# One decoder layer on one core: scan chunks in one block, choice, scores and time steps in one block, constants behind the first weights

## The reference

```python
z, xbc, dt_raw, q_raw, k_raw, v_raw, iq_raw, ik, iw_raw, g_a, g_b = split_cols(rms_norm(x, norm1_g) @ w_in)
# (A) state space branch: depthwise causal conv of 4 taps and silu on x/B/C, then
dt = softplus(dt_raw + dt_bias); A = -exp(a_log)
# prompt, in chunks of 128 positions, h carried from chunk to chunk, per group g and head r:
acum = cumsum(dt * A); lmat = exp(where(causal, acum_t - acum_s, -inf)); cb = C @ B.T
y = (cb * lmat * dt) @ x + exp(acum) * (C @ h)
h = h * exp(acum[-1]) + B.T @ (exp(acum[-1] - acum) * dt * x)
# samples: one step, h = h * exp(dt * A) + dt * x * B, y = C . h
y_ssd = group_rms_norm((y + d_skip * x) * silu(z))
# (B) sparse attention: indexer scores pick the keys of each query
score = sum_h iw_h * relu(iq_h . ik) / 8, masked to k_pos <= q_pos
idx = top_k(score, 64 for the prompt, 256 for a sample)
y_att = softmax(q . k[idx] / 8 + rel_bias[bucket(distance)]) @ v[idx]
# merge, then 8 heads x 16 of 16384 single-neuron experts
x = x + (sigmoid(g_a) * (y_ssd @ w_a) + sigmoid(g_b) * (y_att @ w_b)) @ w_out
out = x + peer(rms_norm(x, norm2_g))
```

## Time and profile before

| | |
|---|---|
| median of 3 executions | 1476.19 us (1475.57 to 1476.94) |
| the profiled execution | 1481.15 us, span 1479.5 us |
| busy, share of the span | PE 1257.2 us (85%), DVE 857.2 (58%), ACT 580.8 (39%), POOL 383.9 (26%) |
| moved by DMA | 391.26 MB, mean 264 GB/s |
| mean granted TensorE clock | 0.95 |

### The profile page before, as it was taken

One profiled execution on the slowest core, in us unless ns is written; L12 is line 12 of the kernel. 1 busy time (PEld: TensorE's weight loads), 2 busy tenths in 40 slices (PEclk: granted clock), 3 DMA queues, 4 the chain that ended last, 5 costly groups with the idle time before them and its releaser, 6 DMA issues. The chain is left out here.

```text
span 1479.5 us, 17316 instructions
## 1 busy us (share of the span) xinstructions
PE 1257.2 (85%) x4988; PEld 770.5 (52%) x4988; DVE 857.2 (58%) x2345; ACT 580.8 (39%) x1542; POOL 383.9 (26%) x510
## 2 busy tenths in 40 slices
PE   5997899999677878889989999877778777777776
PEld 4876578777555557758867555322223222222221
DVE  1044369998284334551116867878965667776444
ACT  1153237878383404320004444343343333333343
POOL 1320012222021110010002445443534334333341
PEclk8998999999796889899999999999999999999999
DMA  4563123334289462123337999999999999999995
GB/s 151 172 214 99 58 93 122 111 103 148 100 285 327 149 232 76 29 72 117 112 127 297 420 421 421 421 420 421 421 422 421 421 421 420 421 421 419 421 413 238
DMA packets 80185, 391.26 MB, mean 264 GB/s; under 512 B 13432, under 2 KB 23192, under 8 KB 43744
## 3 DMA queue, kind: packets, MB, share of 16 engines
q0 software_dynamic: 43104, 287.92, 47.5%
q1 hardware_dynamic: 36016, 100.68, 19.9%
q10 hardware_dynamic: 976, 1.61, 0.3%
HBM read 378.43 MB, written 11.60 MB: 264 GB/s over the span
## 5 line engine op out<-in xcount | busy, mean ns | idle before, releaser
L2039 DVE CUSTOM_DVE_ANT_0 pe_uv<-pe_uv,pe_hnat 128x1024 f32<-128x1024 f32 x264 | 322.9, 1223 | 195.4 <-DMA pe_uv<-d_uv,pe_idx 180.5
L1899 POOL DMA_INDIRECT pe_uv<-d_uv,pe_idx x256 | 268.0, 1047 | 398.4 <-PE pe_acc L1776 184.3
L1776 PE MATMUL pe_ph<-pe_uv,pe_dg 128*128 128x512 f32 x512 | 253.0, 618 | 69.8 <-ACT pe_dg L1843 69.8
L1776 PE MATMUL pe_acc<-pe_uv,pe_dg 128*128 128x512 f32 (+1 forms) x544 | 257.8, 610 | 49.3 <-ACT pe_dg L1843 49.3
L181 PE MATMUL pi_ps<-xn,pi_w 128*128 128x264 f32 x944 | 228.3, 399 | 9.5 <-PEq L87 9.5
L1776 PEld LDWEIGHTS pe_ph<-pe_uv,pe_dg 128*128 128x128 f32 x512 | 87.0, 189 | 235.3 <-ACT pe_dg L1843 173.1
L181 PEld LDWEIGHTS pi_ps<-xn,pi_w 128*128 128x128 f32 x944 | 183.5, 198 | 42.8 <-issue 11.3
L1837 ACT ACTIVATE pe_gl<-pe_a 128x1 f32<-128x1 f32 x264 | 53.4, 202 | 379.0 <-DVE pe_a L2039 378.5
L1776 PEld LDWEIGHTS pe_acc<-pe_uv,pe_dg 128*128 128x128 f32 (+1 forms) x544 | 93.7, 184 | 205.0 <-ACT pe_dg L1843 118.2
L1843 ACT ACTIVATE pe_dg<-cst,pe_w 128x128 f32<-128x128 f32 x256 | 102.7, 401 | 8.3
L1840 ACT ACTIVATE pe_w<-pe_gl,pe_gw 128x1 f32<-128x1 f32 x256 | 75.4, 295 | 8.3
(11 more groups left out here) (296 smaller groups left out, 1655.9 us busy)
## 6 DMA issues: line engine op xcount, KB each, us to landing
pi_w<-d_w_in SPq DMA_DIRECT2D x71, 512.0 KB, 3.5
mw_w<-d_w_ab SPq DMA_DIRECT2D x24, 512.0 KB, 3.7
ss_h<-d_state SPq DMA_DIRECT2D x8, 1024.0 KB, 6.9
o_ssm_s<-ss_h SPq DMA_DIRECT2D x8, 1024.0 KB, 7.0
pq_w<-d_wq SPq DMA_DIRECT2D x16, 512.0 KB, 7.7
paged<-d_ck POOLq DMA_DIRECT2D x40, 128.0 KB, 3.3
lg_w<-d_w_in SPq DMA_DIRECT2D x10, 512.0 KB, 6.4
paged<-d_cv POOLq DMA_DIRECT2D x32, 128.0 KB, 4.9
```

What stands on the lines that cost most here:

```text
L1776: mm = pe.matmul(accs[n][0:m, 4 * half:4 * half + 4, :], lhsT, uv[:, r, D_MODEL + half * 512:D_MODEL + (half + 1) * 512], start=False, sto ...
L1899: pool.indirect_dma_start(uv[:, r, :], None, k.d_uv[:], bass.IndirectOffsetOnAxis(ap=src, axis=0)).then_inc(gathered[r], 16)
L2039: dve.tensor_tensor_reduce(uv[:, r, 0:D_MODEL], uv[:, r, 0:D_MODEL], hnat[:, n, :], 1.0, 0.0, ALU.mult, ALU.add, a[:, r:r + 1]).then_inc(d ...
```

## The change

Seven edits, all ahead of the merge:

1. `norm_in` becomes part of `project_attention`. x is loaded in 4 parts with a semaphore each, squared on DVE part by part, summed by PE with a ones tile that DVE fills; ACT loads the root's table with a one-element activation; PE's first tile waits for each normalised chunk, not for all 8. `cst` is loaded behind the first 4 weight tiles, `cx` and the gain from ACT's queue. ACT's six tables and POOL's pages are issued in the same block, so from its start.
2. The z and x/B/C tiles come in a fixed mixed order (7 z, 4 x, 3 z, 28 x, 6 z); the host reorders the weights.
3. `prepare_attention` takes 7 tiles, loads the time steps' three tables, and no longer waits for the stored keys, values and indexer keys; `attend_prompt` does.
4. `choose_prompt`, `score_sample` and `time_steps` become one block, `choose`, with 7 tiles; the widening is one matmul of 256 columns on a table of products that DVE makes. Its scratch and the bias tables of the samples lie in the room of `gate`.
5. `attend_prompt` has 34 tiles, one in each of its 32 steps and two at its tail, and loads the samples' bias tables.
6. `attend_sample`: 16 gate tiles, 4 of them in the key phase at visits 3, 6, 9 and 12, 2 between, 10 over the value visits.
7. `ssd_chunk` twice becomes `scan` once, with 16 groups; chunk 1's transposes and products are made in chunk 0's groups 2 to 7 and in chunk 1's first two, in one PSUM bank, the attention tiles come at every third group.

The core of the diff:

```diff
-N_LAST = 10
+N_LAST, N_KEYS = 16, 4
+COLUMNS = "z" * 7 + "x" * 4 + "z" * 3 + "x" * 28 + "z" * 6
...
 def project_attention(nc, k):
+            for i in range(PARTS):
+                sp.dma_start(k.xT[:, i * WIDE:(i + 1) * WIDE, :], k.d_xT[:, i * WIDE:(i + 1) * WIDE, :]
+                             ).then_inc(x_loaded[i], 16)
+            for n in range(WSLOTS):
+                pj.load(sp, n)
+            sp.dma_start(k.cst[:], k.d_cst[:]).then_inc(c_loaded, 16)
...
+            for c in range(KD):
+                if c % WIDE == 0:
+                    pe.wait_ge(squared, c // WIDE + 1)
+                mm = pe.matmul(sums[:, 0:T], one[:], xsq[:, c, :], start=c == 0, stop=c == KD - 1)
...
-                pj.multiply(pe, n)
+                pj.multiply(pe, n, (lambda c: pe.wait_ge(done, c + 1)) if n == 0 else None)
...
+            act.wait_ge(filled, 2)
+            act.activation(warm[:, 1:2], warm[:, 0:1], ACT.Sqrt).then_inc(warmed, 1)
...
 def prepare_attention(nc, k, tiles):
-            sp.wait_ge(stored, 48)
...
+def choose(nc, k, tiles):
+            k.proj.multiply(pe, tail[0])
+            pe.wait_ge(rectified, len(steps))
...
+            k.proj.multiply(pe, tail[1])
...
+                if b == 1:
+                    pe.wait_ge(diag, TS)
+                if b:
+                    scores(b - 1)
+                if b == 5:
+                    pe.wait_ge(s_weighed, 2)
+                    pe.wait_ge(dA_ready, 1)
+                    pe.matmul(cum[:, 0:NP_], k.tri, k.dA[:, 0:NP_], start=True, stop=True)
...
+            k.proj.multiply(pe, tail[2])
...
+            pe.matmul(px, k.half_of, k.ts["each"][rows, :], start=True, stop=True,
+                      tile_position=(DT_P, 0)).then_inc(widened, 1)
...
+            for step in range(STEPS):
...
+                for tile in beside[step]:
+                    k.proj.convolve(dve, tile)
+                if step == 1:
+                    dve.wait_ge(e_ready, 1)
+                    dve.tensor_scalar(u, e, 1.0, None, ALU.add).then_inc(u_ready, 1)
...
+                if step == 4:
+                    dve.wait_ge(spread, 1)
+                    for b in range(TS):
+                        dve.tensor_copy(iqd[:, b, b * IH:(b + 1) * IH],
...
 def attend_prompt(nc, k, tiles):
-        share = shares(tiles, N) + [[]] * LAG_O
+        share = shares(tiles[:-2], N) + [[], tiles[-2:-1], tiles[-1:]]
+            sp.dma_start(k.as_hot, k.d_hots[:]).then_inc(k.bias_loaded, 16)
+            sp.dma_start(k.as_rel, k.d_relbh[:]).then_inc(k.bias_loaded, 16)
...
+            sp.wait_ge(k.pa_stored, 48)
...
 def attend_sample(nc, k):
-        after = [[]] * VK + [[0, 1]] + shares(range(2, N_LAST), TS)
+        after = ([[(t - 3) // 3] if t % 3 == 0 and 3 <= t < 3 + 3 * N_KEYS else [] for t in range(VK)]
+                 + [[N_KEYS, N_KEYS + 1]] + shares(range(N_KEYS + 2, N_LAST), TS))
-        weights_at = [VK + NG + 1 if t == VK else VK + NG + 2 * (t - VK) for t in turn]
+        weights_at = [t + NG + 1 if t <= VK else VK + NG + 2 * (t - VK) for t in turn]
...
-                if VK - gates.SLOTS <= visit < VK:
-                    gates.load(sp, visit - VK + gates.SLOTS)
+                if visit - NG < gates.SLOTS:
+                    gates.load(sp, visit - NG)
...
+                if n % 2 == 1 and n // 2 < VK:
+                    for g in after[n // 2]:
+                        gates.multiply(pe, g)
...
+def scan(nc, k, mw):
+        beside = {3 * i: i for i in range(mw.AHEAD)}
+        second = {2: ("x", 0), 3: ("b", 0), 4: ("x", 1), 5: ("cb", 0), 6: ("x", 2), 7: ("b", 1), 8: ("x", 3), 9: ("cb", 1)}
...
+                if m in beside:
+                    mw.attention(pe, beside[m], tr[:, 1, 0:T])
+                prepare(m)
...
+                kind, n = second.get(m - 1, ("", 0))
+                if kind == "x":
+                    drain(1, n, 0, 6 + (1, 3, 4, 6)[n])
```

More of the change, by code:

```diff
@@ L305, in project_attention @@
         table, = (sem("table"),)
+        xsq, g1, rms, one, warm = tensors(nc, ctx, n1_xsq=(P, KD, T), n1_g=(P, KD), n1_rms=(P, T), n1_one=(P, P),
+                                          n1_warm=(P, 2))
+        sums = ctx.enter_context(nc.psum_tensor("n1_ps", [P, 512], F32))
+        PARTS, WIDE = 4, KD // 4
+        x_loaded = [sem(f"n1_x{i}") for i in range(PARTS)]
+        c_loaded, eps_loaded, squared, summed, rooted, inverted, done, filled, warmed = (sem("n1_" + n) for n in (
+            "c", "eps", "sq", "sum", "root", "inv", "done", "one", "warm"))
         block = ctx.enter_context(nc.Block())
@@ L507, in _ @@
                     k.proj.multiply(pe, tile)
-            for tile in tail:
-                k.proj.multiply(pe, tile)
+            k.proj.multiply(pe, tail[0])
+            pe.wait_ge(rectified, len(steps))
+            for h in range(IH):
+                pe.matmul(small[:, h * TS:(h + 1) * TS], k.selhi if h % 2 else k.sello,
+                          k.att[:, IQ0 + h // 2, TP:T], start=True, stop=True)
+            pe.matmul(small[0:TS * IH, 128:128 + TS], k.iwsel, k.misc[:, TP:T], start=True, stop=True
+                      ).then_inc(spread, 1)
@@ L569, in _ @@
                                    pattern=[[-1, P]], channel_multiplier=1).then_inc(cut, 1)
+            for tile in tail:
+                k.proj.tails(pool, tile)
             for i in range(2):
@@ L783, in _ @@
                     k.proj.convolve(dve, tile)
+            assert not any(t - 2 in X_AT for t in tiles[-2:])
             dve.wait_ge(replaced, N)
@@ L998, in _, with turn, cross @@
+        heads = lambda a, c, h0, n: a[:, c * SSDH + h0:c * SSDH + h0 + n]
+        columns = lambda c: slice(c * P, c * P + P)
+        state = lambda g: slice(g * 4 * HD, (g + 1) * 4 * HD)
+        beside = {3 * i: i for i in range(mw.AHEAD)}
+        assert max(beside) < N
+        second = {2: ("x", 0), 3: ("b", 0), 4: ("x", 1), 5: ("cb", 0), 6: ("x", 2), 7: ("b", 1), 8: ("x", 3), 9: ("cb", 1)}
         @block.tensor
         def _(pe):
+            def turn(c, n, bank):
+                for i in range(4):
+                    mm = pe.transpose(tr[:, bank, i * P:(i + 1) * P], k.xbc[:, 4 * n + i, columns(c)], k.ident)
+                mm.then_inc(turned, 1)
+            def cross(c, n, bank):
+                for i in range(4):
+                    g = 4 * n + i
+                    mm = pe.matmul(tr[:, bank, i * P:(i + 1) * P], k.xbc[:, KI + g, columns(c)],
+                                   k.xbc[:, KI + GROUPS + g, columns(c)], start=True, stop=True)
+                mm.then_inc(crossed, 1)
@@ L1462, in _ @@
                     ssd.fade(act, n // 2)
+                if n % 2 == 0 and n:
+                    for g in after[n // 2 - 1]:
+                        gates.evacuate(act, g)
             for g in after[VK]:
```

749 lines of the change are left out of this document (363 added, 386 removed).

## The result

The changed kernel takes a median of **1414.53 us** (1413.84 to 1416.82, 4 executions), the old one beside it 1476.57: a ratio of 0.9573, 95% interval [0.9543, 0.9604], that is 62 us less. The forecast was 40 us less, 1436, with a range that began at 1425: right in sign, two thirds of what came, and outside its range.

The account below looks back on a forecast made before the run. The DMA-bound expert stage streams at its limit, so front-part savings, timed mostly on PE, come off the end: -8.8 + 1.6 - 3.3 - 35.5 + 13.5 - 7.7 = -40.2, from 1476.19 to a median of 1436 us; range 1425 to 1450.

Parts of the forecast that it names:

- The start: Up to the first projection matmul: earlier sums, early root table, chunk-by-chunk feed and no barrier save 8.8 us.
- choosing with its stall: Choosing block: one tile fewer and no first barrier, but PE stalls about 5 us on DVE's copies; -3.3 us.
- prompt attention with the time steps: Time steps leave the path (22.5 us), attention has four tiles fewer (14.5), 1.5 given back: -35.5 us.
- Rival (c): Start: x's four parts land later than one, first matmul at 18, only -4.9 there; 1440 us, chance 0.07.
- (d): Sample attention: gate loads waiting in SP's in-order queue block state loads and stores; slower, 1485 us, chance 0.03.
- Rival (e): More gain: no stall on copies, gates in DMA's waits; -53, 1423 us, likelier half of it, 1428; chance 0.07.
- the expert stage streams rows at the limit, the change leaves it alone: Last stage: DMA-bound at 410 GB/s and unchanged (0 us), so time saved earlier comes off the end one for one.
- -7.7: Scan: the 16.3 us between chunks goes, part is given back inside the loop; bounds -12 (no stall) to -4.
- the terms given back: Scan loop: 5.2 us for transposes and products, 3 for stalls, 0.4 at the moved attention tiles.
- +13.5: Sample attention, longer by moved gate tiles and weights; bounds +7 (gates sink into DMA waits) and +23 (delays add).
- the key phase's +8: Sample attention: gate tiles delaying DVE's state chain, overlapping their transfers, +6 us; lost hiding by the bias preload, +2.
- the value phase's +5.5: Sample attention: two more gate tiles cost 7.6 us, partly taken up by PE's 13.1 us idle; +5.5.

Follow-up runs that it names:

- e12: Kernel before with only the constant table `cx` widened from 256 to 272 columns, moving later SBUF tensors by 64 bytes: 1466.2 us, ratio 0.9934.
- e17: Changed kernel with `cx` 320 columns wide instead of 272, putting the gather's ring back at remainder 192 of 256: 1426.14 us, ratio 0.9643.
- e20: Changed kernel with the scan's six attention tiles back at groups 1, 3, 5 of each chunk: 1419.97 us, ratio 0.9634.
- e5: Changed kernel without the key phase's four gate tiles and their weight loads, outputs copied from other tiles: 1409.8 us, ratio 0.9559.
- e11: Changed kernel with each gate tile's weights issued two visits earlier: 1414.91 us, ratio 0.9588.
- e18: Changed kernel with DVE's copies after the third top-k step instead of the fifth and gate weights issued two visits earlier: 1409.65 us, ratio 0.9535.
- e19: Changed kernel, unedited, measured and profiled a third time: 1415.09 us, ratio 0.9576.

## Why the prediction was right or wrong

**Right.** The method held: what the front part lost came off the end. The start (-8.3 for -8.8), preparing, choosing with its stall, and prompt attention with the time steps (-35.9 for -35.5) came out as costed. In the stretch behind the copies the terms add up to 22.2, not 21.9, which changes nothing. Rival (c) was right that four parts are whole later than one (7.44 for 6.30), but not in its price: sums start at 4.97 and the first matmul comes at 14.60, not 18. Of (d), the blocked queue, there is no sign: the key phase is no longer than before. Rival (e) named the right side, and one cause that came true, the gates in the DMA's waits; but the ring is not in it, and of the scan's surplus only 1.3.

**Wrong: "the expert stage streams rows at the limit, the change leaves it alone".** This first step failed. The code is untouched, but a table made wider ahead of it moved the ring by 64 bytes onto a 256-byte boundary, and the stage that the prediction itself called bound by transfers streams 1.4% faster. The sum lacks a term of about -10 (-11.3 in the table's pair); e12 and e17 show it in both kernels and both directions. The earlier trace rows tell only that 410 GB/s was the rate, not that it was the limit.

**Wrong in size: the scan's "-7.7".** The stretch between the chunks went as forecast, 16.3. What failed are the terms given back: 5.2 + 3 + 0.4 = 8.6 were put in, and opening and loops together grew by 1.1 (from 85.1 to 86.2). The stalls of 3 are 1.25 and 0.34, both on ACT's drain of `bnat`; the 0.4 for the moved tiles was a gain of about 4 (e20), since a tile at group 0 fills a wait of PE. -15.2, and -13.9 between the means, lie outside the bounds of -12 to -4; the -12, which by its own terms is -11.1, had no case in which moving tiles helps.

**Wrong in its parts: sample attention's "+13.5".** The sum is inside the bounds, +8.3 in the pair and +11.1 between the means, but that is partly luck, two errors of opposite sign: the key phase's +8 was -2.6 in the pair and nothing between the means, and the value phase's +5.5 was +11. The key phase step added tile times to DVE's chain; by e5's profile that chain itself waits for the loads of the states, and the tiles sink for the most part into these waits, which was the lower bound. The value phase step assumed that PE's idle time would take part of two tiles; instead PE is 8.1 busier and idle 2.9 longer, with 6.1 of waits for weights where the old profile's rows show one of 1.08. Weights issued earlier make the value phase some 5 shorter (e11, e18), but no median shows that the kernel gains by it.

**Small and open.** The merge's -3.3 was not in the sum. Kernels with the old scan take 116.2 to 116.9 for it, those with the new one 113.6 to 115.6 and once 116.3. It seems to go with the granted clock in the merge's first 30 us; the windows view of its second 10 us, before and after:

```profile
659.75:669.75 10.00, 9.37 (x32) 6.20 (x31) 3.66 (x9) 0.00 (x0) 0.00 (x0) 0.82 0.23 80
607.00:617.00 10.00, 9.37 (x39) 6.68 (x39) 4.10 (x10) 0.00 (x0) 0.00 (x0) 1.00 0.27 93
```

In the unedited kernel's third profile (e19), with a merge of 115.3, these 10 us had 0.72. So the clock there varies from execution to execution with the same code, and only part of the 3.3, if any, is the change's.

The two profiles, then, differ by 27 more than forecast: 11.3 in the expert stage, 7.5 in the scan, 5.2 in sample attention, 3.3 in the merge; the other terms cancel. The medians differ by 22 more than forecast, since the old profile lay 4.6 over its median and the new one 0.7 under; the means over all profiles put the ring at 10, the scan at 6 and sample attention at 2 of it. What of the remaining few is the clock and what the change is open.

## What to carry to other kernels

When a change resizes any tensor, compare the addresses of the tiles that a transfer-bound stage writes to: a stage whose code is untouched can still change, and here 64 bytes were worth 10 us. Extra work placed in waits for transfers can be nearly free (four tiles of 3.8 left the key phase as long as it was); but its own weights are transfers too, and fetching them earlier shortened one phase here without a gain that the medians show. When the order of work moves, look for waits that the moved pieces fill, not only for delays that they add.
